# Moving two thirds of the first U-tile remainders from VectorE to GpSimd in a two-layer expert decoder trunk

## The reference

```python
def peer(h, w_query, sub_keys, u_tab, v_tab):        # 16384 experts, 8 heads, top 16 of each
    q = (xt @ w_query).reshape(T, N_RET_HEADS, 2, HALF_KEY)
    s = jnp.einsum('thpd,hpnd->thpn', q, sub_keys)
    s_half, i_half = lax.top_k(s, TOPK_HALF)
    cand_s = s_half[:, :, 0, :, None] + s_half[:, :, 1, None, :]
    ...
    top_s, pos = lax.top_k(cand_s, TOPK)
    ids = jnp.take_along_axis(cand_i, pos, axis=-1)
    gates = jax.nn.softmax(top_s, axis=-1)
    a = jax.nn.gelu(jnp.einsum('chkd,cd->chk', u_tab[idc], xc))
    coef = gc * a
    return jnp.einsum('chk,chkd->cd', coef, v_tab[idc])
```

## Time and profile before

| | |
|---|---|
| median of three runs | 3477.5 us |
| profiled execution | 3496.24 us, its span 3494.4 us |
| TensorE busy | 3328.6 us (95%) |
| VectorE busy | 2984.3 us (85%) |
| ScalarE busy | 2191.8 us (63%) |
| GpSimd busy | 1330.3 us (38%) |
| DMA | mean 249 GB/s over the span |

### The profile page before, as it was taken

How to read it: one execution, slowest core, us unless ns; L and a number is a source line. 1 busy time by engine, 2 the same in 40 slices (tenths; PEclk the granted TensorE clock), 3 DMA queues, 4 the chain that set the end, 5 groups by cost and what they waited for, 6 DMA issues and landing times.

```text
span 3494.4 us, 63120 instructions
## 1 busy us (share of the span) xinstructions
PE 3328.6 (95%) x19278; PEld 2443.3 (70%) x19278; DVE 2984.3 (85%) x6039; ACT 2191.8 (63%) x3118; POOL 1330.3 (38%) x1126
## 2 busy tenths in 40 slices
PE   6999999999999999999989999999999998999999
PEld 5767775667777667767777677666677776676776
DVE  6899777998888778888869997789988886888888
ACT  3574435567777666777746724455677776766776
POOL 0000017316555556557500000271265564555554
PEclk9999999999999999999999999999999999999999
DMA  5312272459999999999923123535699999999998
GB/s 199 103 61 69 89 264 97 156 190 326 363 354 331 319 353 345 363 350 359 339 81 90 61 79 121 211 115 179 221 335 361 345 341 310 360 355 351 344 361 296
DMA packets 421669, 868.89 MB, mean 249 GB/s; under 512 B 167824, under 2 KB 233360, under 8 KB 421008
## 3 DMA queue, kind: packets, MB, share of 16 engines
q1 hardware_dynamic: 310512, 544.87, 46.3%
q0 software_dynamic: 73728, 268.47, 21.3%
q10 hardware_dynamic: 37152, 52.45, 4.1%
HBM read 774.41 MB, written 85.98 MB: 246 GB/s over the span
## 4 chain that ended last, share of the span: by engine, by line
PE 40%; issue 26%; DVE 15%; POOL 10%; DMA 4%; ACT 3%; DVEq 0%; POOLq 0%; SPq 0%; ACTq 0%
PE ps L924 9%; PE ps L927 8%; PE ps L928 8%; POOL gbuf L586 6%; POOL spare L600 5%; PE ps L636 4%; PE ps L638 3%; PE ps L637 3%; DVE yT L1506 3%; DVE i L1752 2%; DMA raw<-stream 2%; DVE v L1748 1%; DVE S_ring L1758 1%; DMA gbuf<-u_rows,ids_u 1%; PE ps L670 1%
## 5 line engine op out<-in xcount | busy, mean ns | idle before, releaser
L670 PE MATMUL ps<-h,w 128*128 128x384 f16 (+1 forms) x2272 | 760.0, 335 | 40.1 <-ACT w L1012 40.0
L671 PE MATMUL ps<-h,w 128*128 128x384 f16 (+1 forms) x2272 | 756.8, 334 | 0.0
L1012 ACT ACTIVATE w<-w_hi 128x1024 f16<-128x1024 f32 x544 | 572.5, 1052 | 286.3 <-DVE w L1934 174.5
L600 POOL TENSOR_TENSOR spare<-spare 128x1 f32<-128x1 f32 x504 | 393.9, 782 | 909.2 <-DVE a_sp L1740 500.9
L927 PE MATMUL ps<-cf,w 128*128 128x384 f16 x2032 | 665.2, 328 | 0.0
L928 PE MATMUL ps<-cf,w 128*128 128x384 f16 x2032 | 662.2, 327 | 0.0
L667 PE MATMUL ps<-h_hi,w_hi 128*128 128x384 f32 (+1 forms) x2272 | 489.9, 357 | 0.0
L924 PE MATMUL ps<-cf_hi,w_hi 128*128 128x384 f32 x2032 | 430.6, 354 | 23.6 <-DVE cf L1928 23.6
L1934 DVE SCALAR_TENSOR_TENSOR w<-raw,w_hi 128x1024 f16<-128x1024 f32 x256 | 313.3, 1224 | 132.8 <-ACT w_hi L1007 113.6
L667 PEld LDWEIGHTS ps<-h_hi,w_hi 128*128 128x128 f32 x2272 | 396.0, 189 | 17.4 <-issue 0.3
L1000 ACT ACTIVATE w_hi<-raw 128x1024 fp32r<-128x1024 f32 x296 | 313.7, 1060 | 144.6 <-DMA raw<-stream 105.5
(11 more groups left out here) (286 smaller groups left out, 6241.7 us busy)
## 6 DMA issues: line engine op xcount, KB each, us to landing
raw<-stream SPq DMA_DIRECT2D x682, 512.0 KB, 5.6
gelu_scratch<-g_out ACTq DMA_DIRECT2D x256, 192.0 KB, 6.0
cg<-gelu_scratch SPq DMA_DIRECT2D x256, 192.0 KB, 6.8
c_scratch<-stage SPq DMA_DIRECT2D x128, 256.0 KB
cg<-c_scratch SPq DMA_DIRECT2D x256, 128.0 KB, 5.7
qT<-ada SPq DMA_DIRECT2D x32, 512.0 KB, 6.2
cgate<-ada SPq DMA_DIRECT2D x32, 512.0 KB, 5.4
w_rows<-ada SPq DMA_DIRECT2D x32, 512.0 KB, 6.4
```

Source lines behind the costliest of these rows:

```text
L600: nc.gpsimd.tensor_tensor(spare[:, 16:17], spare[:, 17:18], spare[:, 18:19], ALU.add).then_inc(room, 1)
L670: nc.tensor.matmul(ps[:, b, 0:n], w16[:, s, 0, c], h16[:, c, 1, t0:T], start=False, stop=False)
L671: mm = nc.tensor.matmul(ps[:, b, 0:n], w16[:, s, 1, c], h16[:, c, 0, t0:T], start=False, stop=c == C - 1)
L1012: nc.scalar.mul(w16[:, s, 1], w_hi[:, s].bitcast(F32), X_DOWN).then_inc(w16_done, 1)
```

## The change

GpSimd makes the remainders of U tiles 0 to 5 and, of tiles 6 to 32, those whose number is no multiple of three: 24 instead of 4 tiles. VectorE makes those of 6, 9, ..., 30 and of all from 33 on. GpSimd counts its remainders in a semaphore of its own (`pool_low`), and ScalarE's half word waits for the one that belongs to the tile; a tile's number in `lo_done` now counts VectorE's remainders alone. VectorE's plan puts a remainder in for tile u when the planned costs have come to 2690 x (u - 5.5) ns. GpSimd's four first gathers are issued between the remainders of tiles 13 and 14, the others after tile 32's. TensorE waits for the routing behind tile 34, and the 48 groups run from tile 36 over 82 tiles (the last again at tile 116). ScalarE's exponential moves from tile 27 to tile 31. Two waits of VectorE and GpSimd on the joint counter are gone.

```diff
-U_ROUTE = 28
-U_POOL = 4
-LOW_EVERY = 3000
-C_FIRST, C_TILES = 33, 85
+U_ROUTE = 32
+POOL_U = (0, 1, 2, 3, 4, 5) + tuple(u for u in range(6, 33) if u % 3)
+RT_TILE = 34
+C_FIRST, C_TILES = 36, 82
-EXP_TILE = 27
+EXP_TILE = 31
+def low_mark(u):
+
+    return 2690 * (u - 5.5)
@@ GpSimd
-                    up = pool.snap(l * (C * 2 + U_POOL) + i - I_QRY + 1)
+                    up = pool.snap(l * NPL + nth + 1)
...
-                                            ALU.subtract).then_inc(lo_done, 1)
+                                            ALU.subtract).then_inc(pool_low, 1)
...
-                pool.wait_ge(lo_done, l * NT + I_QRY + 4)
-                nc.gpsimd.tensor_tensor(spare[:, 15:16], spare[:, 17:18], spare[:, 18:19], ALU.add)
...
-                for u in range(U_POOL):
-                    low16(u % 4, I_U + u)
-                pool.wait_ge(ids_in, l + 1)
-                pool.wait_ge(row_used, l * 2 * P + SLOTS)
...
+                for nth, u in enumerate(POOL_U):
+                    low16(u % 4, I_U + u, 2 * C + nth)
+                    if u == 13:
+                        pool.wait_ge(ids_in, l + 1)
+                        pool.wait_ge(row_used, l * 2 * P + SLOTS)
+                        nc.gpsimd.tensor_tensor(spare[:, 14:15], spare[:, 17:18], spare[:, 18:19], ALU.add)
+                        for n in range(SLOTS):
+                            gather(n)
+                        gathers = SLOTS
+                for n in range(gathers, 2 * P):
+                    next_gather(n)
@@ TensorE
-                    if u == U_ROUTE + 2:
+                    if u == RT_TILE:
                         pe.wait_ge(rt_ready, l + 1)
@@ ScalarE
                 def half_word_at(i):
 
-                    half_word(i % 4, l * NT + i)
+                    if pooled(i):
+                        half_word(i % 4, pool_low, l * NPL + pool_lows_to(i))
+                    else:
+                        half_word(i % 4, lo_done, l * NL + lows_to(i) + 4)
@@ VectorE
-                lows = [U_POOL]
-                spent = [LOW_EVERY]
+                own_lows = [u for u in range(NKEYS) if u not in POOL_U]
+                spent = [0]
...
-                    if ns and spent[0] >= LOW_EVERY:
-                        spent[0] -= LOW_EVERY
+                    if ns and spent[0] >= low_mark(own_lows[0]):
...
                         u_low()
...
-                dve.wait_ge(lo_done, l * NT + I_U + U_POOL + 4)
-                nc.vector.memset(spare[:, 0:1], 0.0)
...
-                while lows[0] < U_ROUTE + 3:
+                while own_lows[0] <= RT_TILE + 1:
                     u_low()
```

More of the change, by code:

```diff
@@ L83, with pooled, lows_to, pool_lows_to @@
 NE = I_W
+NPL = 2 * C + len(POOL_U)
+NL = NT - NPL
+def pooled(i):
+    return I_QRY <= i < I_U or i - I_U in POOL_U
+def lows_to(i):
+    return sum(not pooled(k) for k in range(i + 1))
+def pool_lows_to(i):
+    return sum(pooled(k) for k in range(i + 1))
 O_GN = 0
@@ L323, in build_trunk @@
         lo_done = sem("lo_done")
+        pool_low = sem("pool_low")
         w16_done = sem("w16_done")
@@ L588, in gather, with next_gather @@
                         in_offset=bass.IndirectOffsetOnAxis(ap=ids[:, k:k + 1], axis=0)).then_inc(row_in[n % SLOTS], 16)
-                for u in range(U_POOL):
-                    low16(u % 4, I_U + u)
-                pool.wait_ge(ids_in, l + 1)
-                pool.wait_ge(row_used, l * 2 * P + SLOTS)
[L594 to L597, removed]
+                def next_gather(n):
                     pool.wait_ge(room, l * (2 * P - SLOTS) + n - SLOTS + 1)
@@ L601, in _ @@
                     gather(n)
+                gathers = 0
+                for nth, u in enumerate(POOL_U):
[9 more added lines that the diff above has]
+                    next_gather(n)
         @block.tensor
@@ L622, in read_no, with product @@
                     return l * (NE // 2) + i // 2 + 2
-                def product(s, g, e, hi, lo, ready=None, chunks=None, t0=0):
+                def product(s, n_low, e, hi, lo, ready=None, chunks=None, t0=0):
                     b, n = s % 2, T - t0
@@ L699, in proj @@
                 def proj(i, hi, lo, chunks=None):
-                    product(i % 4, l * NT + i, l * (NE // 2) + i // 2 + 1, hi, lo, chunks=chunks)
+                    product(i % 4, l * NL + i, l * (NE // 2) + i // 2 + 1, hi, lo, chunks=chunks)
                 def proj_loop(i0, i1, hi, lo, ready=None):
@@ L1722, in mark @@
                     spent[0] += ns
-                    if ns and spent[0] >= LOW_EVERY:
-                        spent[0] -= LOW_EVERY
+                    if ns and spent[0] >= low_mark(own_lows[0]):
+                        routed_rows = route_dots(own_lows[0])
                         u_low()
+                        for k in range(routed_rows):
+                            if dots[0] == 0:
+                                dve.wait_ge(h_ev, 2 * l + 2)
+                            dot()
                 def settle():
@@ L1866, in _ @@
                 assert count[0] == TOP_STEPS, count[0]
-                while lows[0] < U_ROUTE + 3:
+                while own_lows[0] <= RT_TILE + 1:
                     u_low()
                 dve.wait_ge(h_ev, 2 * l + 2)
-                for n in range(DOTS_FIRST):
+                while dots[0] < DOTS_FIRST:
                     dot()
-                    if n == 1:
+                    if dots[0] == DOTS_FIRST - 1:
                         u_low()
@@ L1890, in _ @@
                 for g in range(GROUPS):
-                    while lows[0] <= min(group_tile(g) + 1, NKEYS - 1):
+                    while own_lows and own_lows[0] <= group_tile(g) + 1:
                         u_low()
```

31 lines of the change are left out of this document (16 added, 15 removed).

## The result

The changed kernel takes 3547.24 us (median of four runs, 3540.0 to 3558.15) where the kernel before took 3479.45 in the same session: ratio 1.0201, 95% interval 1.0165 to 1.0236. It is slower, as forecast, but by 68 us instead of 31, and outside the range of 3464 to 3532. The profiled execution took 3558.15 us, its span is 3556.3.

A forecast was written before the change was run, and what follows sets the result against it. VectorE was taken to bound the kernel before tile 36, with DMA nearly full after it. Later tile 36 (+11.1 us) and groups (+4.3) gave +15.4 per layer, +31 for both: about 3509 us, range 3464 to 3532.

The forecast's parts named there:

- What bounds it: Before tile 36 VectorE's remainders pace TensorE, 11.5 us lost; tiles 36 to 118 lose 14.5 us with DMA nearly full.
- Part 1: Routing: VectorE makes 11 remainders instead of 27, 32.8 becomes 13.4 us; gain at most 11.5 us per layer.
- Part 2: Remainders on GpSimd take 4.25 us a tile, 85.0 us for 20 tiles, keeping pace with about a microsecond to spare.
- Part 3: Routing: GpSimd and VectorE's two-operand instructions exclude each other; 61 instructions wait 0.8 us each, 49 us, ending at 796.8.
- Where it reaches TensorE: Tile 34: VectorE's late routing and the gathers put its end at 801, so tile 36 begins at 806, +11.1 us.
- Part 4: Tile 14: the first four gathers ahead of its remainder make TensorE stand 5 us, range 0 to 10.
- Part 5: Tiles 36 to 118: two displaced groups cost 4.3 us per layer, between 2.1 and 9.4; stretch 394 to 398 us.
- Full alternation: Rival, routing: every two-operand instruction waits, 58 us; +18 to +29 us per layer, 3514 to 3535 us; chance 0.20.
- The ports hardly matter: Rival, tiles 6 to 34: at most 0.45 us lost per VectorE instruction; 3468 down to 3459 us; chance 0.20.
- a draw: Rival, routing: exclusion packed almost gaplessly, ending at 788 to 792; 3470 to 3487 us; chance 0.14.
- the first thing named as proof: Sign in the new trace: VectorE's 4096-element comparisons, 2.29 us before, read 3 to 4.5 us.

The follow-up runs named there:

- e2: Changed kernel with GpSimd making only the remainders of tiles 0 to 5, VectorE all others, and the first gathers behind tile 5: 3497.98 us, ratio 1.0034.
- e1: Kernel before with only the coefficient groups moved, to start at tile 36 over 82 tiles instead of 33 over 85: 3503.39 us, ratio 1.0057.
- e3: Changed kernel with GpSimd's two instructions per tile from tile 4 on replaced by fills that read nothing, those remainders left out: 3506.4 us, ratio 1.0060.
- e4: Changed kernel with GpSimd's four first gathers issued behind tile 17's remainder instead of tile 13's: 3541.9 us, ratio 1.0156.
- e6: Kernel before with 16 extra GpSimd products per layer behind tile 3's remainder that nobody waits for: 3505.77 us, ratio 1.0074.
- e7: Kernel before with VectorE's remainders per 2700 ns of counted work instead of 3000, none beyond tile 30, exponential two tiles later: 3482.41 us, ratio 0.9997.
- f1: e2 with only half of each gelu output stored, so it doesn't compute the reference: 3487.34 us, ratio 1.0012.
- f2: e2 with VectorE's one_i comparison made for the first two groups only, so it doesn't compute the reference: 3468.58 us, ratio 0.9959.
- g3: e2 with 104 instead of 114 row products spread over the groups, ten moved behind the last group: 3498.87 us, ratio 1.0046.
- h1: Kernel before with its groups over 91 tiles (33 to 122) instead of 85 (33 to 116): 3491.11 us, ratio 1.0019.

## Why the prediction was wrong, step by step

**What bounds it, and Part 1 (the gain's bound of 11.5 us per layer): right.** e2 has 10 of it: 147.6 against e1's 157.5, both without the two groups.

**Part 2 (GpSimd 4.25 us a tile): right** where it met nobody, 1.90 and 2.37 us at 777.50. What I called "a microsecond of slack" was gone as soon as a product took 3.94 and a difference 4.27 us (at 753.35 and 757.37, tile 26's pair).

**Part 3 (exclusion): right in mechanism and nearly in sum, with another split.** Against the earlier trace rows, the two-operand groups above lengthened by 12 x 0.491 (remainders) + 12 x 0.700 + 4 x 1.535 + 4 x 0.394 + 8 x 0.745 + 4 x 0.927 + 4 x 1.069 + 4 x 0.850 = 39.4 us in 52 instructions: 0.76 each, where I took 0.8. But there are also one-operand instructions, which I had left out. Casts went from 425 to 1647 and from 285 to 828 ns (4 x 1.222 + 4 x 0.543 = 7.1 us), the cast of `parts` gave 1.7, and the single copy of `esum` 2.2: 11.0 us. Two of them on VectorE's timeline, and GpSimd beside them (before: 0.22 and 0.19 us):

```profile
786.06 1.93 DVE L1838 CAST parts<-p 128x128 f32<-128x128 uint32 x1
788.03 2.37 DVE L1841 COPY esum<-t 128x32 f32<-128x32 f32 x1
```
```profile
786.02 1.89 POOL L587 TENSOR_TENSOR raw<-raw,con 128x1024 f32<-128x1024 f32 x1 [4.17 <-ACT w_hi L1033]
787.99 2.36 POOL L590 TENSOR_TENSOR w<-raw,w_hi 128x1024 f16<-128x1024 f32 x1
```

Each lasts as long as GpSimd's instruction. That fits the half of the Trainium skill's rule (SBUF — State Buffer, SBUF: two separate sides) that no row of before showed: a VectorE instruction in a two-port mode takes the lock too. The trace agrees, and the page was right where I left it out of the sum; it further limits the lock of two-input instructions to GpSimd instructions that read SBUF, and e3's rows agree with that as well. The gates came at 804.20, against my 796.8. The waits, 50.4 us against my 49, are not what makes up the 7.4 between: 3.1 are there already at block 0's first candidates (655.05 against 651.92), where tile 0 is 0.9 us later and a 128x8 sum ahead of them took 1.73 us instead of 0.17. The rest is open.

**Where it reaches TensorE: wrong.** I let the loss enter at one place, the routing's end behind tile 34. TensorE never waited for it; its transposes follow tile 34's products with no idle time noted:

```profile
803.97 0.34 PE L703 MATMUL ps<-h,w 128*128 128x384 f16 x1
806.58 1.15 PE L942 MATMUL ps<-con,routed 128*128 128x128 f32 x9
```

(the first row is the first of tile 34's sixteen). It stood, by the gaps ahead of its 16-bit products in the first layer, 5.81 us at tile 12, 3.62 at 14, 3.60 at 26, 3.55 at 30, and 4.4 in five smaller ones: 21.0 in all. At 12 and 30, divisible by three, the late one is VectorE's *own* remainder. The plan puts it in when so many ns of counted work are done (`low_mark`), and the count doesn't know of waits, so each microsecond of exclusion makes the next own remainder a microsecond later for TensorE, while GpSimd, with its four slots full, idles for the next high part (3.0 to 4.2 us at a time). Against e2's 147.6 the 175.3 us are these 21.0 and 6.7 more, of which the products at the lower clock behind the long stands are the part that I can see: the sixteen took 4.77 instead of 2.45 us at tiles 12 and 30, 3.8 at 14 and 4.1 at 26, 7.6 us in all (the gaps and this overlap a little). The clock was in no term of mine. Still this half was +15.6 and +13.4 against +11.1 forecast: 7 of the 29 us by which the profiles' second and first stretches together (60) pass the forecast (31).

**Part 4 (gathers): right**, 3.62 us at tile 14 against 5 in a range of 0 to 10; GpSimd waited for the numbers as feared, and in e4 a stand of 3.79 us went with the gathers.

**Part 5 (groups from tile 36): wrong, and it is the step that failed.** I priced the two displaced groups and the denser ones at 4.3 us, between 2.1 and 9.4, and expected 394 to 398; it is 408.4 and 406.7, +15.5 per layer, the other 22 of those 29 us. e1 gives the edit alone 5.2 and 9.6 us in the stretch (10 against the mean of the six stretches that run before's program) and 20 us in the whole: the upper bound, which I had turned down because only 14.5 us were being lost. The rest, some 8 us per layer, goes with VectorE's missing lead, which had no term at all. Before, its routing ended 132 us behind tile 0 and tile 36 began at 160; it used the 28 us for four row products, two groups and gates. After, it ended at 168 and tile 36 began at 175. In the first layer the kernels with a lead of 26 to 28 us (before, e6, e7, and e1 with its groups moved) take 385 to 398 us in the second stretch. Those with the groups over the same 82 tiles and a lead of 7 to 8 us take 405.6 (e2), 406.5 (e3), 407.3 (e4) and 408.4 (changed); f1, f2 and g3 are left aside, since they take work or bytes out of the stretch. e2 loses the lead with hardly a collision, so the short lead comes with the whole rearrangement and not with the exclusion alone. That it causes the 8 us is argued from this order and from the waits below; no run changes the lead alone. The waits in the second stretch (us in total, times, longest):

```profile
PE ps L928 <- DVE gated_lo L1936: 11.0, 7, 3.8
```
```profile
PE ps L895 <- DVE gated_lo L1899: 1.8, 3, 0.7
```

above after, below before. With how much VectorE has to do in the second stretch goes its length, roughly: busy and stretch are 315.4 and 375.5 in h1, 332.1 and 392.6 before, 341.5 and 397.8 in e1, 346.9 and 406.5 in e3, 347.2 and 408.4 after; the difference is 56 to 61. It is no law: e7 has 332.2 and 384.7 (53), e6 54, g3 55, e2 63, and f2 has 320.7 and 398.4 (78). What moves with a group is also TensorE's, ScalarE's and DMA work, and f2, which takes VectorE's alone, shows that between a third and two thirds of its microseconds count (7.3 of 21.5 and 11.9 of 20.8 in the stretches, 29 of 42 by the medians). How the rest divides is open; an experiment with VectorE's row products taken out while their gathers stay wasn't made.

**The rivals.** "Full alternation" had the size of the routing (+16 to +20) nearly, and its 2.1 to 9 behind it too small as well, so its 3514 to 3535 would also have missed. "The ports hardly matter" and "a draw" fell: the comparisons read 4.33 us, the first thing named as proof.

## What to carry to other kernels

Before work is moved from VectorE to GpSimd, list what VectorE runs meanwhile. As these runs show it, each instruction there with two tensor operands, and each cast or copy, can wait for a whole GpSimd instruction; here the two-operand ones waited 0.76 us each on the average. Then ask not when the moved work ends but who has a place in between: pacing by counted work passes each wait on to the consumer. And a gain at one marker (a tile, a stage) is worth nothing until the next stage's marker moves as well: g3 and h1 were 10 to 18 us early in one stretch and not faster in the end, because the V stage waited 18.5 and 11.7 us for VectorE's coefficients.

## What the runs showed that I had not expected

- A 16-element cast of VectorE (0.16 us) takes 1.1 us on the average beside GpSimd's fills, while 4096-element two-operand comparisons beside the same fills keep their 2.29 us.
- Where VectorE runs two-operand instructions in a row, they alternate: 4.33 (waited one GpSimd instruction), 2.29 (didn't), while GpSimd's own takes 3.94 and 4.27 instead of 1.89 and 2.37. The loser is blocked for the whole instruction of the other.
- Four stands of TensorE, of 3.5 to 5.8 us, cost it a second time. Behind the longest its next products started each 0.32 us instead of 0.16, at a granted clock of 0.63 to 0.68 around them.
